# Decode stage of a hybrid decoder step: score, V-product and turning steps of three page groups placed directly behind each other on TensorE

## The reference

```python
def _fox_sample(q, k_new, v_new, logf_new, cache_k, cache_v, cache_logf, page_table):
    k_past = cache_k[page_table].reshape(Bd, P, H, hd)
    v_past = cache_v[page_table].reshape(Bd, P, H, hd)
    ...
    s_past = jnp.einsum('bqhd,bkhd->bhqk', q, k_past).astype(jnp.float32) * FOX_SCALE
    s_past = s_past + c_q - c_past.transpose(0, 2, 1)[:, :, None, :]
    s_new = jnp.einsum('bqhd,bkhd->bhqk', q, k_new).astype(jnp.float32) * FOX_SCALE
    ...
    p = jax.nn.softmax(jnp.concatenate([s_past, s_new], axis=-1), axis=-1)
    o = (jnp.einsum('bhqk,bkhd->bqhd', p[..., :P].astype(v_past.dtype), v_past)
         + jnp.einsum('bhqk,bkhd->bqhd', p[..., P:].astype(v_new.dtype), v_new))
    return o
```

## Time and profile before

| | |
|---|---|
| median of 3 runs | 1593.81 us (1592.14 to 1604.89) |
| the profiled execution | 1588.89 us, its span 1587.2 us |
| PE busy | 1447.4 us, 91% of the span |
| PE weight loads busy | 1226.6 us, 77% |
| DVE, ACT, POOL busy | 726.3, 565.3, 528.7 us |
| mean granted TensorE clock | 0.972 of full speed |
| moved by DMA | 250.51 MB, mean 158 GB/s |

### The profile page before, as it was taken

The page is one execution under the profiler, slowest core; times in us unless marked ns, Lnnn a source line. Parts: engine busy times, 40 slices in busy tenths (PEclk is TensorE's granted clock), DMA queues, the critical chain, the costliest instruction groups (busy, mean ns, idle before and its releaser), DMA issues. The chain is left out here.

```text
span 1587.2 us, 43486 instructions
## 1 busy us (share of the span) xinstructions
PE 1447.4 (91%) x16281; PEld 1226.6 (77%) x16281; DVE 726.3 (46%) x1578; ACT 565.3 (36%) x1311; POOL 528.7 (33%) x953
## 2 busy tenths in 40 slices
PE   5999898989978897999989999889998899999998
PEld 5878777777767876788877888768876798888876
DVE  4344353543636555655546545655554223333221
ACT  6343444444532334323443334423334353111100
POOL 4444434440047135344353534454251122111000
PEclk9989999999989999999999999989999999999999
DMA  5131301222238688899997999879985764321521
GB/s 173 32 85 34 85 24 54 72 58 68 55 114 212 189 233 216 225 238 235 239 248 206 263 244 243 219 217 244 231 198 158 224 249 139 108 101 62 167 92 60
DMA packets 153411, 250.51 MB, mean 158 GB/s; under 512 B 45897, under 2 KB 58826, under 8 KB 152690
## 3 DMA queue, kind: packets, MB, share of 16 engines
q1 hardware_dynamic: 121618, 215.68, 49.8%
q0 software_dynamic: 31584, 32.04, 7.3%
HBM read 217.37 MB, written 30.22 MB: 156 GB/s over the span
## 5 line engine op out<-in xcount | busy, mean ns | idle before, releaser
L289 PE MATMUL psum<-h_hi,w_hi 128*128 128x384 f32 (+1 forms) x1344 | 491.0, 365 | 13.8 <-DVE q_fm L915 3.5
L289 PE MATMUL psum<-h_hi,w_lo 128*128 128x384 f32 (+1 forms) x1344 | 446.9, 332 | 0.0
L289 PE MATMUL psum<-h_lo,w_hi 128*128 128x384 f32 (+1 forms) x1344 | 446.4, 332 | 0.0
L1457 POOL DMA_DIRECT2D sc<-tmp_bias x512 | 278.3, 549 | 256.7 <-PE psum L1943 252.6
L289 PEld LDWEIGHTS psum<-h_hi,w_hi 128*128 128x128 f32 x1344 | 258.3, 192 | 67.1 <-issue 48.0
L289 PEld LDWEIGHTS psum<-h_lo,w_hi 128*128 128x128 f32 x1344 | 259.4, 193 | 2.7 <-issue 0.5
L289 PEld LDWEIGHTS psum<-h_hi,w_lo 128*128 128x128 f32 x1344 | 257.9, 192 | 0.0
L678 POOL DMA_DIRECT2D lfp<-in_cache_logf x256 | 124.1, 485 | 176.1 <-issue 176.1
L1671 DVE STREAM_TRANSPOSE k_page<-k_page 128x1024 f32<-128x1024 f32 x128 | 156.1, 1232 | 28.8 <-DMA k_page<-in_cache_k 27.8
L264 DVE TENSOR_TENSOR w_lo<-w_raw,w_hi 128x1024 fp32r<-128x1024 f32 x63 | 76.8, 1219 | 110.6 <-ACT w_hi L259 110.5
L259 ACT ACTIVATE w_hi<-w_raw 128x1024 fp32r<-128x1024 f32 x63 | 66.1, 1049 | 69.3 <-DMA w_raw<-in_w_tiles 37.9
(11 more groups left out here) (259 smaller groups left out, 2142.4 us busy)
## 6 DMA issues: line engine op xcount, KB each, us to landing
k_page<-in_cache_k SPq DMA_DIRECT2D x256, 256.0 KB, 3.8
v_page<-in_cache_v SPq DMA_DIRECT2D x256, 256.0 KB, 4.9
w_raw<-in_w_tiles SPq DMA_DIRECT2D x63, 512.0 KB, 5.6
g_pair<-tmp_gates SPq DMA_DIRECT2D x16, 544.0 KB, 4.6
sc<-tmp_bias POOLq DMA_DIRECT2D x512, 16.0 KB, 4.4
tmp_ogla<-gate POOLq DMA_DIRECT2D x4, 1088.0 KB, 6.8
g_pair<-tmp_ogla SPq DMA_DIRECT2D x8, 544.0 KB, 7.3
x_in<-in_x_prompt SPq DMA_DIRECT2D x8, 512.0 KB, 6.1
```

The lines of the kernel that those rows point to most:

```text
L289: m = pe.matmul(out, wt[:, s, k, :], h[:, k, t0:t0 + w], start=(k == 0 and a == 0), stop=(k == KT_ - 1 and a == 2))
L1457: pool.dma_start(dst, src.unsqueeze(0).to_broadcast([TS, 2, 256])).then_inc(sc_in[j % SLOTS], 16)
```

## The change

In each round m of `decode_steps()` the steps `sc`, `pv` and `pt` are gathered in a list `burst` and written one behind the other, with their summed cost at the last, so that `schedule()` places GLA steps only behind the whole burst. In round 0 the burst is `sc`, `new`, `soft`, `exp`, `vn_load` of sequence a, `pv` and `pt` of sequence b, `qbd` and `ql` of sequence s. The steps themselves, their number and their summed cost are the same; `prep` comes behind the burst.

```diff
         for m in range(NPG // 4):
             if has_k:
                 out += [(("kt", s, 2 * m + j), 0.6) for j in range(2)]
-            if m == 0:
-                if has_b:
-                    out.append((("pt", b, NPG // 4 - 1), 0.25))
-                if has_a:
-                    out += [(("sc", a, NPG // 4 - 1), 1.0), (("new", a), 0.2), (("soft", a), 0), (("exp", a), 0), (("vn_load", a), 0)]
-                if has_k and s >= 1:
-                    out += [(("qbd", s), 0), (("ql", s), 0.3)]
-            else:
-                if has_k:
-                    out.append((("sc", s, m - 1), 1.0))
-                if has_a:
-                    out.append((("pt", a, m - 1), 0.25))
+            burst = []
+            if m == 0 and has_a:
+                burst += [(("sc", a, NPG // 4 - 1), 1.0), (("new", a), 0.2), (("soft", a), 0), (("exp", a), 0), (("vn_load", a), 0)]
+            if m and has_k:
+                burst.append((("sc", s, m - 1), 1.0))
+            if m <= 1 and has_b:
+                burst.append((("pv", b, NPG // 4 - 2 + m), 1.1))
+            if m >= 2 and has_a:
+                burst.append((("pv", a, m - 2), 1.1))
+            if m == 0 and has_b:
+                burst.append((("pt", b, NPG // 4 - 1), 0.25))
+            if m and has_a:
+                burst.append((("pt", a, m - 1), 0.25))
+            if m == 0 and has_k and s >= 1:
+                burst += [(("qbd", s), 0), (("ql", s), 0.3)]
+            cost = sum(c for _, c in burst)
+            out += [(step, cost if k == len(burst) - 1 else 0) for k, (step, _) in enumerate(burst)]
             if m % 2 == 0 and s:
                 out.append((("prep", s * SP + m // 2), 0))
-            if m <= 1 and has_b:
-                out.append((("pv", b, NPG // 4 - 2 + m), 1.1))
-            if m >= 2 and has_a:
-                out.append((("pv", a, m - 2), 1.1))
```

## The result

The changed kernel takes 1675.81 us as the median of 4 runs (1670.64 to 1679.57), against 1594.47 us for the kernel before beside it (1592.14 to 1604.89, 4 runs): 1.0495 times as long, interval 1.0439 to 1.055. The profiled execution took 1677.67 us with a span of 1676.0 us, 88.8 us more than the 1587.2 us of before. The forecast was 1645 us with a range of 1615 to 1673: the direction is right, the loss is 81 us where I gave 51, and the result lies just above the range.

What follows compares the result with a forecast made beforehand. PE's own stream was taken as the path; -11 (switches) + 8 (`new`) + 33 (`ql`) + 12 (clock) + 10 (code) = +52 us gave 1641 us profiled, 1645 us median, range 1615 to 1673.

Steps and rivals of the forecast that it cites:

- What bounds the kernel: PE, busy 91% of the span: its own stream is the path, and its stops reach the end almost one for one.
- rival 4: Stops on PE are absorbed by slack elsewhere, gain and loss cancel within 1%, 1578 to 1610 us; chance 0.06.
- rival 3: Faster: `ql` does not wait, as ACT's copy of `pt` precedes the exponentials; 1578 us, median 1582; chance 0.03.
- rival 1: Waits come as counted, but the clock stays up (+3) and code costs nothing more; 1622 us, median 1626; chance 0.18.
- Switches, -11: `sc` directly ahead of `pv`, or of `new` and `pv`, saves 55 x 0.2 = 11 us; bounds 8 and 18.
- `ql` waits, +33: In stages 2 to 7 `ql` waits for ACT's copy of `pt` behind `exp`: 6 x 5.5 = 33 us; bounds 27, 39.
- `new` waits, +8: At 8 stage openings `new`, directly behind `sc`, waits 1.1 us for DVE (line 1688): +8 us, 6 to 14.
- Clock, +12: PE's granted clock falls behind six stops of 5.5 us, 2.4 us each: +12 us; bounds 3 and 20.
- Code, +10: Dense `sc`, `pv`, `pt` make PE stop for code, 13 stops at 1.4 us: +10 us; bounds -8 and +28.
- rival 2: Every code packet holding a burst stops PE by 2.8 us: code +28, clock +20; 1667 us, median 1671; chance 0.07.

Runs made afterwards that it cites:

- filled wait: Changed kernel with 22 unneeded 128x128 matmuls on PE ahead of each of the six waits of `ql`: 1657.44 against 1596.57 us for the kernel before, 1.0384.
- thin bursts: Changed order without its round 0 waits, half of the `sc` and `pv` matmuls left out: 1576.17 us, 0.9859 of the full kernel before.

## Why the prediction was right and wrong

**What bounds the kernel: right.** PE's idle time and its lower clock together rose by 102.5 us and the span by 88.8; the difference is about what the switches give. Nothing absorbed the loss, so rival 4 falls, and the copy of `pt` comes behind the exponentials, so rival 3 falls. The clock fell and code cost more, so rival 1 falls.

**Switches, -11: near.** Starts of `sc` and `pv` are 0.92 us apart, not the 1.03 that I had put down as the mark of no gap. By the earlier trace rows a lone run costs 0.08 on entry, 1.04, and 0.09 behind it, so two lone runs cost 2.42 us and a pair 0.08 + 0.92 + 1.04 + 0.09 = 2.13; an estimate by that is 0.29 for each of the 55, 16 us, where I had 0.2. The rest of the ledger gives -13.7, within the bounds of 8 and 18, but it is a remainder and no measurement of its own, and the thin bursts did not show it.

**`ql` waits, +33: right.** Six waits, 30.3 us, each step of the chain within 0.3 us of the count. Moving `pt` ahead of `sc` took them away.

**`new` waits, +8: too small, the mechanism right.** Eight waits; six of them are 1.13 to 1.41 us, as counted. The other two are 3.79 and 4.11 us. PE and DVE around the longest, in the changed kernel:

```profile
1169.90 1.10 PE L1925 MATMUL psum<-k_page,q_row 128*32 128x64 f32 x64
1175.11 0.41 PE L1935 MATMUL psum<-kn,q_bd 128*32 128x8 f32 x16 [4.11 <-DVE sc_new L1689]
```

```profile
1170.78 1.23 DVE L264 TENSOR_TENSOR w_lo<-w_raw,w_hi 128x1024 fp32r<-128x1024 f32 x1 [4.31 <-ACT w_hi L259]
1171.93 2.36 DVE L1672 STREAM_TRANSPOSE k_page<-k_page 128x1024 f32<-128x1024 f32 x2
1174.21 0.38 DVE L1689 CUSTOM_DVE_ANT_0 sc<-psum,sc 128x256 f32<-128x256 f32 x1
```

DVE had three operations of 1.2 us ahead of line 1689, one of them late because of ACT. My upper bound allowed for half a transpose each time and for none of the cases where DVE comes to its list late. Measured +14.1, the bound was 14.

**Clock, +12: too small.** The rule read from the earlier trace rows, that a stop of several microseconds is followed by a stretch at half pace, held, and the filled wait gives 2.1 us for a wait of `ql` where I had 2.4, 12.6 us for the six. What failed is the count: I let the clock fall behind the six waits of `ql` only. It also fell behind stops for code and the two long waits of `new`, as at 920.02 us above. All together gave +24.2.

**Code, +10: the step that failed most.** That PE waits for its packets of code was right, and now each stop can be laid beside the landing of its packet. The price was not. I took 1.4 us for a stop. The 13 stops of the ledger that lie at limits came to 36.4 us, 2.8 each, which is the 2.78 us of the earlier trace rows that I had set as the upper bound, and the term to +28.3 instead of +10. The prediction had the better number at hand: its own four stops, 7.8 us, are 1.95 each, and 13 of those less 8 would have been +17.

The count of 13 came out by luck. It was to be the limits whose 256 instructions pass in less than 4.7 us. Between 455 and 1360 us the changed kernel has 12 such packets, and 7 of them end without a stop. Of its 14 stops over 0.6 us at limits (39.0 us, the one at 661.96 us with them) 5 end such a packet. The other nine end packets that lasted 4.9 to 11.1 us, and the two packets under 4.7 us of before had no stop, while its four stops end packets of 4.9 to 5.6 us. So the length of a packet alone does not tell where PE stops. In the nine the next packet of code started late, 4.8 to 10.9 us after the limit before, where half of all packets start within 1.8 us; the DMA engines' share in these gaps was 0.75 to 1.05, as in the row above. So the page and weight loads may hold the code up, but no run tests it, and other packets of code started on time with the engines as full.

The Trainium skill, "Runtime: NRT & Kernel Launch", section on instruction fetch mechanics, says that crossing a block is mostly hidden. The thin bursts agree (1 stop, 0.7 us), and in the changed kernel 82 of the 96 limits between 455 and 1360 us do too; the other 14 do not, and they are 39.0 us.

Code and clock together came out at +52.5 where I had +22, and these are the terms of rival 2 (+28 and +20). The result is that rival, at 1671, with the two late waits of `new` on top. I had given it 7 in 100 with the argument that the stop of 1.05 us spoke for a low price; but the four stops of before stand at the same kind of place and are, from start to start, 1.15, 1.26, 3.00 and 3.29 us, so one short one was no ground for a low mean. Rival 2 has every packet that holds a burst stop PE, and that did not happen: 7 of the 12 shortest did not.

**What stays open.** Why some packets of code start late, and with it why one stop costs 0.8 us and another 4.5: a run with the same order and fewer page loads could tell. Moving the limits by 128 instructions changed the stops by 10 us, the lower clock by 19 and the time by some 35. The gain of the switches alone was not shown.

## What to carry to other kernels

When steps are put closer together on the engine that is the path, count for each step what the ones now behind it wait for on the other engines, in the order of their lists: an activation that stood ahead of a softmax and now stands behind it cost 30 us in six places. Count instructions too: where 256 small matmuls and weight loads stood in a row the engine stopped in the middle of them for its code, and one or two pieces of large matmuls between two such runs took three quarters of that loss away. When a trace holds a few stops of one kind, price the next ones by their mean and not by the shortest. A wait taken away may only uncover the next one, so size the one beneath before counting a gain.

## What the runs showed of the hardware

- PE stopped for 0.7 to 5 us at a grid of 256 instructions, in which every matmul record, weight load and semaphore instruction counts, and went on 1.2 to 1.9 us after its packet of code had landed (119 stops in 14 kernels). Most were in runs of small matmuls, one of 3.10 us in a piece of large ones.
- 128 instructions more moved the stops to other steps, the changed kernel by about 35 us and the kernel before by no more than the noise. A comparison of two orders with such runs is therefore uncertain by tens of us until the limits are moved.
- A semaphore increment on PE costs 0.15 us: 128 of them 19.6 us.
- `pv` directly behind `sc`, both on four column tiles, starts 0.92 us after it; alone each takes 1.04 us with its switches.
- Filling six waits of 5 us with idle matmuls kept the clock up behind them: 27.6 us of work at the lower level became 0, an estimated 12.6 us.
